# Down products of the first block's feed-forwards with tokens on partitions, and the second token half turned into the up banks

## The reference, cut to what matters

```python
def swiglu(h, w13, w2):                       # first block, f = 0..3
    a, b = jnp.split(h @ w13, 2, axis=-1)
    return (jax.nn.silu(a) * b) @ w2
...
x = x + 0.5 * g1[:, None] * swiglu(h, ff_w13[l, 0], ff_w2[l, 0])

def _half_ffn(x, g_pre, g_post, w_gate, w_up, w_down):   # second block, f = 4..7
    h = _rmsnorm(x, g_pre)
    f = (jax.nn.silu(h @ w_gate) * (h @ w_up)) @ w_down
    return x + 0.5 * _rmsnorm(f, g_post)
```

## Time and profile before

| | us |
|---|---|
| median of 3 runs | 2169.89 |
| lowest, highest | 2168.46, 2170.3 |
| the profiled execution | 2171.11 |
| its span on the core | 2169.3 |
| PE busy in the span | 2108.2 (97%) |
| DVE busy in the span | 1474.7 (68%) |

### The profile page before, as it was taken

How to read it: one execution, slowest core, us unless ns; L and a number is a source line. 1 busy time by engine, 2 the same in 40 slices (tenths; PEclk the granted TensorE clock), 3 DMA queues, 4 the chain that set the end, 5 groups by cost and what they waited for, 6 DMA issues and landing times.

```text
span 2169.3 us, 31245 instructions
## 1 busy us (share of the span) xinstructions
PE 2108.2 (97%) x12235; PEld 1839.3 (85%) x12249; DVE 1474.7 (68%) x2059; ACT 1002.6 (46%) x1415; POOL 30.0 (1%) x33
## 2 busy tenths in 40 slices
PE   7999999999999999999999999999999999999998
PEld 5888998888888988888888878878887888988887
DVE  6888878888888647674565457975457546677444
ACT  3434545344443555444353446464345445555443
POOL 0000000000000000000000000010000000001000
PEclk9999999999999999999999999999999999999999
DMA  8788445886787431275545543126554553425552
GB/s 340 297 311 304 166 170 214 318 307 245 290 300 261 155 137 60 80 270 180 187 160 190 192 155 111 65 97 212 177 192 156 193 182 147 156 79 175 194 178 93
DMA packets 75606, 417.46 MB, mean 192 GB/s; under 512 B 5888, under 2 KB 6016, under 8 KB 51840
## 3 DMA queue, kind: packets, MB, share of 16 engines
q1 hardware_dynamic: 75520, 416.27, 53.5%
HBM read 415.20 MB, written 1.05 MB: 192 GB/s over the span
## 4 chain that ended last, share of the span: by engine, by line
PE 89%; DVE 7%; ACT 2%; DMA 1%; issue 1%; SPq 0%; DVEq 0%; ACTq 0%
PE AB L748 13%; PE AB L750 13%; PE AB L749 13%; PE Y L293 9%; PE Y L295 9%; PE Y L294 9%; PE AB L293 2%; PE AB L294 2%; PE AB L295 2%; PE Y L1367 2%; DVE lo L2064 2%; PE N L791 2%; PE M L690 1%; PE Y L748 1%; PE Y L750 1%; PE Y L749 1%
## 5 line engine op out<-in xcount | busy, mean ns | idle before, releaser
L2064 DVE TENSOR_TENSOR lo<-raw,hi 128x2048 fp32r<-128x2048 f32 x310 | 708.1, 2286 | 387.3 <-ACT hi L1517 386.9
L1517 ACT ACTIVATE hi<-raw 128x2048 fp32r<-128x2048 f32 x322 | 615.1, 1914 | 544.6 <-PE Y L295 260.2
L748 PE MATMUL AB<-hi,h_hi 128*128 128x512 f32 x1280 | 506.4, 396 | 1.3 <-DVE lo L2064 1.3
L750 PE MATMUL AB<-hi,h_lo 128*128 128x512 f32 x1280 | 499.2, 390 | 0.0
L749 PE MATMUL AB<-lo,h_hi 128*128 128x512 f32 x1280 | 498.3, 389 | 0.0
L750 PEld LDWEIGHTS AB<-hi,h_lo 128*128 128x128 f32 x1280 | 240.2, 188 | 51.3
L748 PEld LDWEIGHTS AB<-hi,h_hi 128*128 128x128 f32 x1280 | 240.5, 188 | 48.9 <-DVE lo L2064 1.5
L749 PEld LDWEIGHTS AB<-lo,h_hi 128*128 128x128 f32 x1280 | 240.7, 188 | 47.9
L293 PE MATMUL Y<-g_hi,hi 128*128 128x256 f32 x664 | 188.2, 283 | 0.0
L294 PE MATMUL Y<-g_lo,hi 128*128 128x256 f32 x664 | 187.9, 283 | 0.0
L295 PE MATMUL Y<-g_hi,lo 128*128 128x256 f32 x664 | 187.8, 283 | 0.0
(11 more groups left out here) (435 smaller groups left out, 3179.1 us busy)
## 6 DMA issues: line engine op xcount, KB each, us to landing
raw<-slabs SPq DMA_DIRECT2D x322, 1024.0 KB, 5.0
ada_raw<-ada SPq DMA_DIRECT2D x34, 2048.0 KB, 8.2
ada_raw<-ada SPq DMA_DIRECT2D x2, 1024.0 KB, 14.6
kT<-ada SPq DMA_DIRECT2D x1, 1024.0 KB, 10.4
vt<-ada SPq DMA_DIRECT2D x1, 1024.0 KB, 12.4
x<-x_t SPq DMA_DIRECT2D x1, 1024.0 KB, 14.4
out_t<-x SPq DMA_DIRECT2D x4, 256.0 KB, 3.0
vec<-vectors SPq DMA_DIRECT2D x1, 462.0 KB, 3.2
```

Of the source, the lines that this page charges most:

```text
L748: nc.tensor.matmul(out_, h_hi[:, k, at], w_hi, start=start, stop=False)
L750: return nc.tensor.matmul(out_, h_lo[:, k, at], w_hi, start=False, stop=stop)
L1517: nc.scalar.activation(hi[slot][:, :], raw[slot][:, :], ACT.Copy).then_inc(hi_done[slot], 1)
L2064: nc.vector.tensor_tensor(lo[slot][:, :], raw[slot][:, :], hi[slot][:, :].bitcast(F32), ALU.subtract).then_inc(lo_done[slot], 1)
```

## The change

All eight FFNs use `down_tok` now. For n = 0, 2, 3, 5 ACT copies `Y` banks 0 and 2 to `kT`, DVE copies banks 1 and 3, PE transposes the four, and DVE adds sixteen 128x128 pieces to `x`. In all eight adds the second token half is transposed into `AB`, with no wait on `x_half`. The halves of the lo split, the variance and the root of the second token half stand earlier on DVE; n = 6, 9 and 11 add the first token half only after the second's copy is scaled. The order of the chunks is 0 to 7 everywhere. `norm` 7 no longer waits for the whole of `x` before its sums. In f = 4 to 7 `square_sum` moves behind the split of the third slab, and the sums of the deferred norm move on PE from ahead of step 1 to behind the first half of its up product; `norm` 9 splits the third slab before it squares.

```diff
@@ -337,7 +337,7 @@
         BANKS = ((0, 1), (2, 3), (4, 5), (6, 7))
         def tail_first(kind, n=6):
-            return n % 3 != 1 if kind == "add" else kind == "final" or 0 < n < 6 and n % 3 != 2
+            return False
         def place(kind, n=6):
             ks = [k for part in (TAIL if tail_first(kind, n) else BANKS) for k in part]
@@ -474,14 +474,18 @@
         ysq = kT
         BY_TOKEN = (6, 8, 9, 11)
+        FFN_ADDS = (0, 2, 3, 5) + BY_TOKEN
         def pair_of(t_, q):
             return t_[:, 2 * q:2 * q + 2, :].rearrange("p k t -> p (k t)")
+        def turn_banks(t):
+            return (M, N) if t == 0 else (AB[:, 0, :], AB[:, 1, :])
+
         def token_bank(eng, c, n, q):
             if q < 3:
-                eng.wait_ge(y_ready, 16 + 3 * BY_TOKEN.index(n) + q + 1)
+                eng.wait_ge(y_ready, 3 * FFN_ADDS.index(n) + q + 1)
             else:
                 last = c["slab"] - c["ahead"] - 1
                 eng.wait_ge(used[last % 3], last // 3 + 1)
@@ -728,7 +732,6 @@
                 if n in DEFERRED:
                     c.take("sq", KD)
                 elif n >= 6:
-                    pe.wait_ge(x_new, X_BEFORE[6] + KD)
                     stat(KD, ones[1024])
                 elif n:
                     if n == 2:
@@ -853,11 +856,11 @@
             def turn_tokens(n, t):
-                i = BY_TOKEN.index(n)
-                for b, bank in enumerate((M, N)):
+                i = FFN_ADDS.index(n)
+                if t == 0:
+                    pe.wait_ge(yt_dve, 2 * i + 1)
+                for b, bank in enumerate(turn_banks(t)):
                     pe.wait_ge((yt_act, yt_dve)[b], 2 * i + t + 1)
-                    if t:
-                        pe.wait_ge(x_half, KD * i + KD // 2 * (b + 1))
                     for kk in range(KD // 2):
                         mm = nc.tensor.transpose(bank[:, kk * P:(kk + 1) * P],
                                                  pair_of(kT, 2 * t + b)[:, kk * P:(kk + 1) * P], ident[:, :])
@@ -887,21 +890,20 @@
             def ffn(f):
                 q0, n_ada = ADA_FFN.get(f, (0, 0))
                 g0 = c.take("g", NSTEP)
-                down = down_tok if f >= 4 else down_features
+                down = down_tok
                 if f == 6:
                     first_up_by_token(8)
                 else:
                     first_up()
-                if f >= 4:
-                    sums([(acc_ready, c.take("acc") + 1, rstd)], ones[1024])
-                    c.take("stat")
-
                 ring = step_slots(c.take("slab", 3 * NSTEP - 3))
                 def step(i, ada, first=False, last=False):
                     pe.wait_ge(lo_done[ring[0][0]], i + (ring[0][1] + 1))
                     up(ring[0][0], 0)
                     if first:
+                        if f >= 4:
+                            sums([(acc_ready, c.take("acc") + 1, rstd)], ones[1024])
+                            c.take("stat")
                         turn_gated(i + g0)
                     pe.wait_ge(lo_done[ring[1][0]], i + (ring[1][1] + 1))
                     up(ring[1][0], 1)
@@ -929,7 +931,7 @@
                 down(j % 3, z_hi, z_lo, last=f // 2 * 3 + f % 2 * 2)
             def add(n):
-                if n in BY_TOKEN:
+                if n in FFN_ADDS:
                     keep_warm(4)
                     turn_tokens(n, 0)
                     if n != 8:
@@ -1565,7 +1567,7 @@
             def rounded_half(n, ks):
                 for k in ks:
-                    act.wait_ge(x_half, KD + k + 1)
+                    act.wait_ge(x_half, KD * FFN_ADDS.index(8) + k + 1)
                     nc.scalar.activation(h_hi[:, k, 0:P], x[:, k, 0:P], ACT.Copy, scale=pre_gain(n)[:, k:k + 1]
                                          ).then_inc(hh_half, 1)
@@ -1578,6 +1580,10 @@
                         act.wait_ge(x_new, c["x_new"] - KD + k + 1)
                         nc.scalar.activation(h_hi[:, k, P:T], x[:, k, P:T], ACT.Copy, scale=g[:, k:k + 1]
                                              ).then_inc(hh_ready, 1)
+                    j = c.take("slab")
+                    split(j % 3, j // 3)
+                    c["ahead"] += 1
+                    for k in range(KD):
                         nc.scalar.activation(hf[:, k, :], x[:, k, :], ACT.Square).then_inc(sq_ready, 1)
                     return
                 if n in DEFERRED:
@@ -1658,6 +1664,11 @@
             def add(n):
                 c.take("x_new", KD)
+                if n in FFN_ADDS and n < 6:
+                    for t in range(TT):
+                        token_bank(act, c, n, 2 * t)
+                        nc.scalar.activation(pair_of(kT, 2 * t), y_bank(2 * t), ACT.Copy).then_inc(yt_act, 1)
+                    return
                 if n in BY_TOKEN:
                     i = BY_TOKEN.index(n)
@@ -2266,7 +2277,8 @@
                 if n in DEFERRED:
                     c.take("hh", KD)
                     c.take("h", KD)
-                    square_sum(n)
+                    if n == 10:
+                        square_sum(n)
                     return
                 if n < 6:
                     l, j = divmod(n, 3)
@@ -2330,6 +2342,7 @@
                 next_slab()
                 next_slab()
                 if f >= 4:
+                    square_sum({4: 6, 5: 8, 6: 9, 7: 11}[f])
                     root_of(EPS)
                     c.take("unspread")
                 j0 = c.take("slab", 3 * NSTEP - 4) - 1
@@ -2372,7 +2385,8 @@
             def by_token_add(n):
-                i = BY_TOKEN.index(n)
+                ia = FFN_ADDS.index(n)
+                i = ia - 4
                 def variance(t):
                     dve.wait_ge(half_squared, 4 * i + 2 * t + 2)
@@ -2394,9 +2408,9 @@
                 def residual(t, *ks):
                     for k in ks:
                         b, kk = divmod(k, KD // 2)
-                        dve.wait_ge(yt_turned, 4 * i + 2 * t + b + 1)
+                        dve.wait_ge(yt_turned, 4 * ia + 2 * t + b + 1)
                         at = slice(t * P, (t + 1) * P)
-                        nc.vector.scalar_tensor_tensor(x[:, k, at], (M, N)[b][:, kk * P:(kk + 1) * P], gate[:, k:k + 1],
+                        nc.vector.scalar_tensor_tensor(x[:, k, at], turn_banks(t)[b][:, kk * P:(kk + 1) * P], gate[:, k:k + 1],
                                                        x[:, k, at], ALU.mult, ALU.add).then_inc(x_new if t else x_half, 1)
                 def low(t, *ks):
@@ -2409,24 +2423,36 @@
                                                        h_hi[:, k, at].bitcast(F32), ALU.mult, ALU.subtract
                                                        ).then_inc(h_ready if t else h_half, 1)
+                if n < 6:
+                    for t in range(TT):
+                        token_bank(dve, c, n, 2 * t + 1)
+                        nc.vector.tensor_copy(pair_of(kT, 2 * t + 1), y_bank(2 * t + 1)).then_inc(yt_dve, 1)
+                        residual(t, *range(KD))
+                        if t == 0:
+                            second_half()
+                    return
                 variance(0)
                 newton(0)
                 second(0)
-                residual(0, 0, 1)
+                second_half()
                 variance(1)
-                low(0, 0)
-                residual(0, 2, 3)
-                low(0, 1)
-                newton(1)
-                second(1)
                 if n == 8:
-                    second_half()
-                low(0, 2, 3)
-                for k in range(4, KD):
-                    residual(0, k)
-                    if k > 4:
-                        low(0, k - 1)
-                low(0, KD - 1)
+                    residual(0, 0, 1)
+                    low(0, 0)
+                    residual(0, 2, 3)
+                    low(0, 1)
+                    newton(1)
+                    second(1)
+                    low(0, 2, 3)
+                    for k in range(4, KD):
+                        residual(0, k)
+                        if k > 4:
+                            low(0, k - 1)
+                    low(0, KD - 1)
+                else:
+                    newton(1)
+                    second(1)
+                    residual(0, *range(KD))
                 for k in range(KD + 1):
                     if k < KD:
                         residual(1, k)
@@ -2434,8 +2460,6 @@
                         low(1, k - 1)
                         if n == 9:
                             low_half(n + 1, k - 1)
-                    if k == 3:
-                        second_half()
             def add(n):
```

## The result

The changed kernel takes 2215.18 us (median of 4 runs, 2212.57 to 2216.08), against 2170.1 for the kernel before on the same chip (2168.46 to 2171.52): a ratio of 1.0206, 95% interval 1.0188 to 1.0224. The forecast was 2217, in a range from 2199 to 2229. The profiled execution took 2214.2 from its first to its last instruction, 44.9 more than the one before (2169.3).

The account below looks back on a forecast made before the run. PE was taken as the bound, busy for 2108 of 2169 us. The terms -13.6 + 30.8 + 7 + 19.3 + 9.2 - 5.0 - 0.3 = +47.4, added to the median of 2169.9, gave 2217 us, range 2199 to 2229.

Parts of the forecast that it names:

- The products: Down products of f = 0 to 3: 44 products go from 5.76 to 5.45 us each, -13.6 us.
- T: At the end of a FFN, the time at which PE goes on behind its last down product.
- that rival (2051): Down products of f = 0 to 3: a matmul costs its duration, 4.1 us gained per product, 2051 us; chance 0.03.
- the rival by which short and long matmuls would take the same (2228): Down products: TensorE keeps the page's gap, 11 us more, 2228; chance 0.10, shared with hand-overs at the top of their bounds.
- The ends of f = 0 to 3: From last down product to next norm: +30.8 us for the longer chain, +7 for half clock, over four places.
- T+10 as its sign: Ends of f = 0 to 3: the tree's sums end at T+10; T+8 would say that the tree hides.
- The rival that squares and additions hide in the residuals: Ends of f = 0 to 3: 6 us go; part of the more-overlap rival, 2201 or 2190; chance 0.10.
- The first steps of f = 4 to 7: PE waits for root, split and gate: +5.1 us for f = 4, 5, 7, +4.0 for f = 6, together +19.3.
- The clock behind these waits: Behind the 5 us waits in f = 4 to 7: half clock costs 2.3 us four times, +9.2, bounds 0 and 12.
- The rival of a clock that holds (2201): Ends of f = 0 to 3 and behind the 5 us waits: clock stays up, 16 us fall away, 2201; chance 0.15.
- Add 6, 9 and 11: Sums of norm 7 start earlier at full clock, -5.0 us in add 6; -0.3 for adds 9 and 11.
- the bound of -3: Add 6: the gain is only 3 us instead of 5.0 if its sums run at half clock again.

Follow-up runs that it names:

- e6: Changed kernel plus zero matmuls at the ends of f = 0 to 3, nine ahead of the last four transposes and five ahead of the sums: 2208.09 us.
- e1: Changed kernel with the deferred norm's sums ahead of step 1 again, DVE's sum of squares ahead of its split, norm 9's split behind ACT's squares: 2186.58 us.
- e7: Changed kernel with only PE's sums back ahead of step 1 in f = 4 to 7; DVE's sum of squares stays behind the split: 2197.34 us.
- e4: Changed kernel plus 22 zero matmuls between the sums and the gated transposes in the first step of f = 4 to 7: 2206.8 us.
- e2: Changed kernel with down product, residual and tail of f = 0 to 3 in the features form again: 2198.41 us; the same kernel run again: 2191.7.

## Why the prediction was right, point by point

**The products.** Forecast -13.6, measured -13.3 with T corrected, of which 0.5 already stand at the first gated transposes of f = 0 and are the clock's at the start (half clock for 3.4 us from 40.6, before for 6.8 us from 37.8). Each product gains 0.30 to 0.32, as the earlier trace rows gave, and the duration of single matmuls meant nothing: that rival (2051) is out. So is the rival by which short and long matmuls would take the same (2228). The Trainium skill (TensorE: Matmul & The Clock Gate, "Back-to-back issue gap") gives 216 ns for 512 columns as the gap of a single matmul taken by itself, and about 131 as the sustained rate of a stream. The trace has 227 for these, which fits neither; the forecast had named only the first of the two figures. Without the 0.5 the term was 0.8 too large, 0.2 a FFN. In the table it looks larger, because the last product, that of z, seems to take 5.67 us to T (from 1111.04 to 1116.71 at f = 3) and not 5.44: that is the missing record.

**The ends of f = 0 to 3.** Forecast 30.8 for the chain and 7 for the clock, together 37.8; measured 37.2. e6, with the clock held, has 31.3 for the chain, so the clock is 5.8: the chain was read within 0.2 us a place, the clock taken 1.2 too high, because at two of the four ends it was at half for 3.4 us only. The steps, counted in e6 from an exact T: first residual at T+1.5 (forecast T+1.3), `x` whole at T+7.5 (T+7.3), POOL's last addition done at T+8.7 (T+8.7), end of the sums at T+10.4 (T+10.2). The forecast took its T+1.3 from the earlier trace rows, whose T is 0.23 late, so it began 0.2 too early. And its text adds two additions of 0.73 to T+6.9 and writes T+8.7, which is 8.4: POOL is still at its first addition then (until T+7.2 in e6), a wait that the text doesn't name and the figure holds. In the changed kernel itself the sums end at T+11.8 where the forecast gave T+10 as its sign: the half clock, which it priced apart, lies in them. The rival that squares and additions hide in the residuals would have had 6 us less.

**The first steps of f = 4 to 7.** Forecast 19.3, measured 19.0, and f = 6 is shorter than the others by 1.8 where 1.1 had been expected. e1 shows it as the part that it undoes. What the forecast took for granted, that DVE's order from root to gate is unchanged, holds; e7 adds that DVE's addition behind the split costs some 11 us even where PE's sums stay ahead, which the forecast didn't separate.

**The clock behind these waits.** Forecast 9.2, measured 7.6 by the difference at T and 8.4 by e4 against the changed kernel. This is the term that was furthest off. The rival of a clock that holds (2201) is out at both places.

**Add 6, 8, 9 and 11.** Forecast -5.3, measured -4.9, 0.0, +0.1 and -0.1. (1299.8 and eight times 0.5 is 1303.8 and not 1303.6, so the rows gave -4.8 for n = 6.) The sums start at T+5.7 (1329.62) and take 3.84 us at full clock; the bound of -3, with half clock again, didn't come here (e7 had half clock in these sums and gained 3.3). Why the clock held in one and not in the other is open.

**What the sum didn't have.** The mixers, in which nothing is changed, differ by -3.7, +2.9, -1.4 and +1.6 us. The trace before has half clock from 321 to 328 in the hybrid mixer, the changed one has none there; in the nsa mixer it has half clock at 876 to 884 and 890 to 894, where the kernel before had only 863 to 867. They cancel to -0.6 here, which is luck: the largest is more than twice the error of any term, and e2 shows 11.6 us of it. Sum of all measured terms: -12.4 + 36.3 + 19.0 + 7.6 - 4.9 - 0.6 = +45.0, the difference of the spans (with T corrected -13.3 and 37.2 stand for the first two, with the same sum). The forecast was 2.4 higher, mostly by the two terms of the clock, 1.2 and 1.6.

## What to carry to other kernels

A product that is 0.3 us shorter eleven times a stage did not pay for a form in which turning, adding and squaring follow the last product in a row: price that chain piece by piece from a place where the form already runs, and look at the helper engine's order in it, which was worth 3 us a place here. A small reduction directly ahead of its consumer exposes all that stands between the two, here 5.2 us that 24 matmuls had covered. Where the bound engine is TensorE, add to each new wait of 2 us and more what the halved clock took behind it, here 1.1 to 2.2 us.

## What the runs showed of the hardware that I had not expected

24 us at half clock with PE busy throughout (773 to 797 us in e2), in a place with no wait ahead of it that the other executions don't have as well; the same kernel had 3.4 us there in another execution. What decides it is open. Where in a mixer the shorter stretches fall shifts from kernel to kernel, so that stages with the same instructions differ by up to 3.7 us: a difference between two kernels is better read stage by stage than by the sum alone.

Zero matmuls in a wait gave the clock back wholly, at both places (1.00 in the stretches behind them in e4 and e6), and cost nothing that can be seen: the waits of e4 were as long as without them.

A trace can lack a record at the very place from which one counts. One zero matmul of four, missing at each end, moved T by 0.23 us: the gain of the products came out 0.9 us too small and the cost of the ends 0.9 too large. Count the instructions of a row against the program before taking its start as a mark.
